# First up phase: four groups on the unnormalised activation, normalised tiles at every second k-tile

## What is computed

```python
def _rmsnorm(x, g):
    y = x32 * lax.rsqrt(jnp.mean(x32 * x32, axis=-1, keepdims=True) + NORM_EPS)
    return (y * g.astype(F32)).astype(x.dtype)

def _conv_ffn(x, w_up, conv_w, conv_b, w_down):
    u = _causal_dwconv(x @ w_up, conv_w, conv_b)      # three taps along the tokens
    gate, up = jnp.split(u, 2, axis=-1)
    return (jax.nn.silu(gate) * up) @ w_down

x = x + mix                                            # attention, ends with @ w_o
x = x + _conv_ffn(_rmsnorm(x, norm_ffn[i]), ffn_w_up[i], ...)
```

## Time and profile before

| what | value |
|---|---|
| median of 3 runs | 819.25 us (818.97 to 820.73) |
| span of the profiled execution | 817.3 us |
| median less span (lead-in and end; the profiled execution has no time of its own beside its span) | 1.95 us |
| TensorE busy | 802.3 us, 98% |
| VectorE busy | 644.4 us, 79% |
| ScalarE busy | 487.0 us, 60% |
| HBM read | 177.27 MB |

### The profile page before, as it was taken

How to read it: one execution, slowest core, us unless ns; L and a number is a source line. 1 busy time by engine, 2 the same in 40 slices (tenths; PEclk the granted TensorE clock), 3 DMA queues, 4 the chain that set the end, 5 groups by cost and what they waited for, 6 DMA issues and landing times.

```text
span 817.3 us, 16917 instructions
## 1 busy us (share of the span) xinstructions
PE 802.3 (98%) x6862; PEld 780.7 (96%) x6862; DVE 644.4 (79%) x1333; ACT 487.0 (60%) x1015; POOL 21.2 (3%) x53
## 2 busy tenths in 40 slices
PE   7999999999999999999999999899999999999998
PEld 7999998999999999999999999889889999999998
DVE  5788887888899887999988786977667896775551
ACT  6754566767767565756554556665655775555440
POOL 1000000000000000000000000700000000000000
PEclk9999999999999999999999999999999999999999
DMA  8777673765565998489998887545334578665540
GB/s 290 260 234 226 200 267 128 235 199 188 189 225 166 324 308 286 144 295 336 361 333 292 288 263 222 167 134 175 120 118 156 156 249 274 207 199 194 194 155 27
DMA packets 150013, 179.44 MB, mean 220 GB/s; under 512 B 5680, under 2 KB 139568, under 8 KB 149936
## 3 DMA queue, kind: packets, MB, share of 16 engines
q1 hardware_dynamic: 147680, 177.22, 65.8%
q10 hardware_dynamic: 1232, 1.11, 0.4%
q0 software_dynamic: 1024, 0.03, 0.1%
HBM read 177.27 MB, written 1.05 MB: 218 GB/s over the span
## 4 chain that ended last, share of the span: by engine, by line
PE 77%; DVE 4%; ACT 2%; issue 1%; DVEq 0%; ACTq 0%
PE bank L1349 24%; PE bank L1352 24%; PE bank L1353 24%; DVE wlo L970 1%; PE bank L1451 1%; PE bank L1439 1%; PE bank L1468 0%; PE bank L1370 0%; PE bank L1402 0%; DVE yb L1010 0%; PE bank L1418 0%; DVE A L1021 0%; ACT B L748 0%; PE bank L1395 0%; ACT sq L768 0%
## 5 line engine op out<-in xcount | busy, mean ns | idle before, releaser
L970 DVE TENSOR_TENSOR wlo<-raw,whi 128x512 fp32r<-128x512 f32 x528 | 342.7, 683 | 69.4 <-ACT whi L727 68.7
L727 ACT ACTIVATE whi<-raw 128x512 fp32r<-128x512 f32 x528 | 307.3, 622 | 97.1 <-PE bank L1353 85.2
L1349 PE MATMUL bank<-A,whi 128*128 128x256 f32 x1264 | 357.3, 283 | 3.4 <-DVE wlo L970 2.6
L1352 PE MATMUL bank<-A,whi 128*128 128x256 f32 x1264 | 350.6, 277 | 0.1
L1353 PE MATMUL bank<-A,wlo 128*128 128x256 f32 x1264 | 350.2, 277 | 0.0
L1349 PEld LDWEIGHTS bank<-A,whi 128*128 128x128 f32 x1264 | 237.7, 188 | 6.5 <-DVE wlo L970 3.5
L1352 PEld LDWEIGHTS bank<-A,whi 128*128 128x128 f32 x1264 | 237.7, 188 | 1.2 <-issue 1.0
L1353 PEld LDWEIGHTS bank<-A,wlo 128*128 128x128 f32 x1264 | 237.8, 188 | 0.0
L1349 PE MATMUL bank<-Hhi,whi 128*128 128x256 f32 x528 | 146.2, 277 | 0.0
L1353 PE MATMUL bank<-Hhi,wlo 128*128 128x256 f32 x528 | 145.9, 276 | 0.0
L1352 PE MATMUL bank<-Hlo,whi 128*128 128x256 f32 x528 | 145.9, 276 | 0.0
(11 more groups left out here) (150 smaller groups left out, 811.0 us busy)
## 6 DMA issues: line engine op xcount, KB each, us to landing
mring<-in_w_mod SPq DMA_DIRECT2D x72, 512.0 KB, 6.4
raw<-in_ffn_w_up SPq DMA_DIRECT2D x22, 1024.0 KB, 5.1
raw<-in_w_gate SPq DMA_DIRECT2D x22, 1024.0 KB, 5.7
raw<-in_w_up SPq DMA_DIRECT2D x22, 1024.0 KB, 6.0
raw<-in_w_down SPq DMA_DIRECT2D x16, 1024.0 KB, 5.4
raw<-in_w_in SPq DMA_DIRECT2D x12, 1024.0 KB, 5.4
raw<-in_moba_w_qkv SPq DMA_DIRECT2D x11, 1024.0 KB, 5.5
raw<-in_ffn_w_down SPq DMA_DIRECT2D x8, 1024.0 KB, 6.2
```

The source lines that it names most:

```text
L727: act.activation(whi[:, i % SPL, k0:k1, 0:width], raw[:, i % RAW, k0:k1, 0:width], ACT.Copy).then_inc(s_whi, 1)
L970: dve.tensor_tensor(lo, raw[:, i % RAW, k0:k1, 0:width], hi.bitcast(F32), ALU.subtract).then_inc(s_wlo, 1)
L1349: pe.matmul(o, hi, xh, start=kg == 0 and not (j and halved(g)), stop=False)
L1352: pe.matmul(o, hi, xl, start=False, stop=False)
```

## The change

Up1 gets the form of the three other phases.

- `RAW_GROUPS` and `RAW_OF` get "up1". The first four groups of up1 (slabs 17 to 20) multiply `B`, 256 columns, filled by "ain" steps behind each residual group of o1.
- The squares of tiles 6 and 7 are one step again, added into `acc` by VectorE; the sum is one step. The second set of fillers is gone.
- The eviction of the first group is deferred to the third k-tile of slab 18, right behind the root's sum. "cg" may now be deferred.
- An unnormalised group is first multiplied by the root, bank to `tmp`, two VectorE instructions. ScalarE's last tap waits for that (`s_scaled`) and all three taps read `tmp`. `s_evicted` is raised where it was, after the taps.
- Normalised tiles: y(0) at k-tile 4 of slab 18, y(1) at k-tile 6, y(2) to y(5) at k-tiles 0, 2, 4, 6 of slab 19, y(6) and y(7) at 0 and 2 of slab 20, each followed by the low part of the tile before. Slab 21 is the first to use them.
- The residuals of down1 also wait for `s_alo` and `s_acc`, since B's low halves and the squares read the same x.

```diff
-RAW_GROUPS = {"up2": 4, "qkv3": 4, "up4": 4}
-RAW_OF = {"up2": 0, "qkv3": 1, "up4": 2}
-LATE_OF = {"up1": 0, "up2": 1, "qkv3": 2, "up4": 3}
+RAW_GROUPS = {"up1": 4, "up2": 4, "qkv3": 4, "up4": 4}
+RAW_OF = {"up1": 0, "up2": 1, "qkv3": 2, "up4": 3}
-WARM = (13, 9)
+WARM = 13
...
-                    if to != "up1":
-                        for n in (c0 // P, c0 // P + 1):
-                            st.put("ain", to, n)
+                    for n in (c0 // P, c0 // P + 1):
+                        st.put("ain", to, n)
                     st.put("sq", to, c0 // C)
...
-                if first and tag not in ("o", "down", "cg"):
+                if first and tag not in ("o", "down"):
                     deferred.append(g)
...
-                if norm == "up1":
-                    st.put("norm", norm)
-                    st.put("warm", 1)
-                    for n in range(KD):
-                        st.put("latey", norm, n)
-                        for m in ([n - 1] if n else []) + ([n] if n == KD - 1 else []):
-                            st.put("latelo", norm, m)
...
+        def up_out(g, i, c0=0, c1=S):
+
+            return tmp[:, (0 if groups[g][1] == "cg" else 2) + i, c0:c1] if g in unnormed else at(g, i, c0, c1)
...
                     if part == 0:
-                        need.wait_ge(s_chunk, chunk_of_group(g))
+                        if g not in unnormed:
+                            need.wait_ge(s_chunk, chunk_of_group(g))
                         need.wait_ge(s_rest, 16)
                         need.wait_ge(s_h1, conv_g[g] // 2)
                         for i in range(2):
                             c = half + 2 * j + i
-                            act.activation(ca[:, sl + i, :], at(g, i), ACT.Identity, bias=cvec[:, 3, c:c + 1],
+                            if g in unnormed:
+                                need.wait_ge(s_scaled, 2 * mul_g[g] - 1 + i)
+                            act.activation(ca[:, sl + i, :], up_out(g, i), ACT.Identity, bias=cvec[:, 3, c:c + 1],
                                            scale=cvec[:, 2, c:c + 1]).then_inc(s_conv0, 1)
...
+                    if part == 0 and g in unnormed:
+                        have_r(ph)
+                        for i in range(2):
+                            dve.tensor_tensor(up_out(g, i), at(g, i), Rr[:, 0, :], ALU.mult).then_inc(s_scaled, 1)
...
                             ins = dve.scalar_tensor_tensor(
-                                out=y[:, part:S], in0=at(g, i, 0, S - part), scalar=cvec[:, 2 - part, c:c + 1],
+                                out=y[:, part:S], in0=up_out(g, i, 0, S - part), scalar=cvec[:, 2 - part, c:c + 1],
...
                 if g in unnormed:
                     need.wait_ge(s_alo, 8 * NORM_OF[ph] + kg + 1)
+                    if ph == "up1":
+                        return Bhi[:, kg, 0:S], Blo[:, kg, 0:S], S
...
-                early = i == plan.first_of["up1"]
-                xh, xl, ncol = here(tag, ph, kg, g, early)
+                xh, xl, ncol = here(tag, ph, kg, g)
```

More of the change, by code:

```diff
@@ L522, in build_program @@
         sq_index = {part: k + 1 for k, part in enumerate(sq_parts)}
-        acc_index = {part: k + 1 for k, part in enumerate(p for p in sq_parts if p[1] > 0 and p != ("up1", 3, 0))}
+        acc_index = {part: k + 1 for k, part in enumerate(p for p in sq_parts if p[1] > 0)}
         conv_g = {g: k for k, g in enumerate(g for g, x in enumerate(groups) if x[1] in ("cg", "cu"))}
@@ L753, in squares @@
                 x_here(ph, 2 * q)
-                if not (ph == "up1" and q == 3):
-                    x_here(ph, 2 * q + 1)
+                x_here(ph, 2 * q + 1)
                 for j in range(2 if ph == "up2" else 1):
@@ L760, in squares @@
                     else:
-                        need.wait_ge(s_acc, acc_index["up1", 2, 0] if ph == "up1" and q == 3 else acc_index[ph, q, j] - 1)
+                        need.wait_ge(s_acc, acc_index[ph, q, j] - 1)
                         o = sq[:, :, :]
[L763 to L767, removed]
+                    if j == 0:
                         act.activation(o, XT[:, 2 * q:2 * q + 2, :], ACT.Square).then_inc(s_sq, 1)
@@ L985, in add_squares @@
             def add_squares(ph, q):
-                if q == 0 or (ph == "up1" and q == 3):
+                if q == 0:
                     return
@@ L997, in late_y @@
                 have_r(ph)
-                k = 8 * LATE_OF[ph] + n
-                if ph == "up1":
-                    emptied(need, res_group("o1", n))
-                    if n >= 4:
-                        need.wait_ge(s_ahi, 8 + n - 3)
-                        need.wait_ge(s_alo, 8 + n - 3)
-                    gain = vec[:, VC["norm_ffn"] + n:VC["norm_ffn"] + n + 1]
-                else:
-                    if n >= 4:
-                        need.wait_ge(s_nhi, 8 * RAW_OF[ph] + n - 3)
-                        need.wait_ge(s_nlo, 8 * RAW_OF[ph] + n - 3)
-                    gain = gcol[:, n:n + 1]
-                dve.scalar_tensor_tensor(out=yb[:, n % 4, :], in0=XT[:, n, :], scalar=gain, in1=Rr[:, 0, :],
+                k = 8 * RAW_OF[ph] + n
+                if n >= 4:
+                    need.wait_ge(s_nhi, 8 * RAW_OF[ph] + n - 3)
+                    need.wait_ge(s_nlo, 8 * RAW_OF[ph] + n - 3)
+                dve.scalar_tensor_tensor(out=yb[:, n % 4, :], in0=XT[:, n, :], scalar=gain_of(ph, n), in1=Rr[:, 0, :],
                                          op0=ALU.mult, op1=ALU.mult).then_inc(s_latey, 1)
@@ L1189, in evict @@
                             need.wait_ge(s_latey, n + 1)
+                            need.wait_ge(s_alo, 8 + n + 1)
+                            need.wait_ge(s_acc, acc_index["up1", 3, 0])
                         elif ph == "down2":
@@ L1303, in _, with here @@
             need = Once(pe)
-            def here(tag, ph, kg, g, high=False):
-                if high:
-                    need.wait_ge(s_ahi, 8 * NORM_OF[ph] + kg + 1)
-                    return Ahi[:, kg, :], Alo[:, kg, :], S
+            def here(tag, ph, kg, g):
                 if tag in ("o", "ot"):
@@ L1349, in multiply @@
                     pe.matmul(o, hi, xh, start=kg == 0 and not (j and halved(g)), stop=False)
-                    if early:
-                        here(tag, ph, kg, g)
                     pe.matmul(o, hi, xl, start=False, stop=False)
@@ L1355, in multiply, with warm @@
                     ins.then_inc(s_chunk, 1)
-            def warm(k):
+            def warm():
                 need.wait_ge(s_const, 3)
-                for _ in range(WARM[k]):
+                for _ in range(WARM):
                     pe.matmul(banks[T_BANK][:, 0:P], meanf[:, :], meanf[:, :], start=True, stop=True)
@@ L1365, in norm @@
                 need.wait_ge(s_const, n_const)
-                late = ph == "up1"
                 for j in range(2 if ph == "up2" else 1):
-                    need.wait_ge(s_acc, acc_index[ph, 2 if late else 3, j])
+                    need.wait_ge(s_acc, acc_index[ph, 3, j])
                     for t in range(2):
-                        ins = pe.matmul(b[:, j * S:(j + 1) * S], meanf[:, :], acc[:, j, t, :], start=t == 0, stop=t == 1 and not late)
-                if late:
-                    need.wait_ge(s_sq, sq_index[ph, 3, 0])
-                    for t in range(2):
-                        ins = pe.matmul(b[:, 0:S], meanf[:, :], sq[:, t, :], start=False, stop=t == 1)
+                        ins = pe.matmul(b[:, j * S:(j + 1) * S], meanf[:, :], acc[:, j, t, :], start=t == 0, stop=t == 1)
                 ins.then_inc(s_sums, 1)
```

27 lines of the change are left out of this document (14 added, 13 removed).

## The result

The changed kernel takes 826.94 us (median of 5 runs, 826.70 to 827.84) where the kernel before took 820.32 beside it (818.97 to 820.73): ratio 1.0087, 95% interval 1.0071 to 1.0102. It is slower by some 7 us, outside the range given.

The account below looks back on a forecast made before the run. TensorE, 98% busy, bounds the kernel, but VectorE's list in up1 sets the end: the seam's 5.8 us come back in the fifth slab, so 819.25 + 0.2 = 819.5 us, range 815.8 to 822.2.

Parts of the forecast that it names:

- The seam: From o1 to up1, B products follow O without a gap, at 127.27, removing 5.82 us without product work.
- rival D: At the tile 5 stall the clock grant falls to 1.2 GHz: +3 us, 822.5; chance 0.08.
- the stall at tile 5: In up1's fifth slab TensorE waits 3.3 us for normalised tile 5, ready at 158.5.
- VectorE's list: VectorE's uninterrupted work in up1 from the root to normalised tile 5: 21.7 us, setting the end.
- The root: Sum matmul in up1's second slab at 134.7; VectorE starts scaling at 136.8.
- Rival B: VectorE passes up1's fifth slab without being late; the seam's 3.4 to 3.8 us stay: 815.7; chance 0.14.
- B slabs: Each of up1's first four slabs, multiplied from B, takes 5.75 us, between ends 5.44 and 5.8.
- rival C: ScalarE's round trips lengthen VectorE's list in up1; with 2.0 us more, 821.5; chance 0.16.
- The waits inside the list: VectorE waits in up1: 1.0 us behind the silu table load, 0.4 for ScalarE's copy in the third group.
- A: VectorE gives back the whole seam gain in up1's fifth slab: 819.5, range 818.2 to 820.9; chance 0.62.
- Banks of the fourth group, weights: After up1's fifth slab: bank emptied about 165.0, wanted 167; seventh-slab weights 3 us early, later loads' lateness hidden.
- The sum: Sixth up1 slab starts at 161.3 to 161.5 against 161.20: change +0.2 us, total 819.5.

Follow-up runs that it names:

- experiment 1: Changed kernel with the bank turn begun at 0 instead of 2, so up1 starts on banks 0 and 1: 823.0 us, ratio 1.0043.
- experiment 2: Changed kernel with the bank turn begun at 1 instead of 2, so up1 starts on banks 2 and 3: 821.87 us, ratio 1.0030.
- experiment 3: Changed kernel, banks as they are, plus 13 filler matmuls ahead of up1's first product: 824.84 us, ratio 1.0069.
- experiment 6: Kernel of experiment 2 without VectorE's convolution taps for the four unnormalised groups (output not the reference's): 819.92 us, ratio 1.0002.
- the table variant: Kernel of experiment 1 with ScalarE's silu table loaded right behind the root, ahead of the first copy: 822.83 us, ratio 1.0045.
- experiment 8: Kernel before without its nine filler matmuls at the o1 to up1 seam: 821.79 us, ratio 1.0026.
- experiment 4: Kernel of experiment 1 with six unnormalised groups in up1 instead of four: 824.19 us, ratio 1.0057.
- experiment 5: Kernel of experiment 2 with up1's normalised tiles made at every k-tile instead of every second: 821.66 us, ratio 1.0031.
- experiment 7: Kernel of experiment 5 with the low half of up1's hidden tiles computed on GpSimd instead of VectorE: 822.70 us, ratio 1.0041.
- the shifted B: Kernel of experiment 5 with the rows of B 272 columns apart instead of 258: 822.35 us, ratio 1.0034.

## Why the prediction failed, point by point

**The seam (the step that failed first).** "The stream could go on at 127.27" took the o3 to up4 seam as price list. Up4 begins with the first pair of banks, which o3's last group does not hold; up1 begins with the pair that o1's last group holds. I did not look up who owned the bank. Experiments 1 and 2 change nothing else and the wait is gone. It costs 3.3 us (130.59 where 127.27 was forecast), and the first fall of the clock came with it.

**The clock (the second).** The forecast took no fall, and gave rival D a chance of 0.08 although it named the place, the stall at tile 5. That fall came in the profiles of the change and of every kernel here whose stall at tile 5 stayed (experiments 1, 2, 3, 6 and the table variant); in experiment 6 a wait of 2.32 us was enough. Its price was overstated: matmuls start 0.21 us apart instead of 0.12 over 3.41 us, so some 1.4 us of work are lost and not 3; experiment 3 gives 1.3. The Trainium skill (TensorE: Matmul & The Clock Gate, Part 1), which the prediction weighed at D, says that an idle array drops to half rate, and the traces agree: 0.50 in or behind waits of 3.17, 3.07 and 3.06 us., on which I leaned, show a wait of 1.93 us only, and experiment 8 shows a fall within waits of 1.19 and 2.03. "The granted clock is 1.00 throughout" was also read too far: the first 4.70 us have no record.

**VectorE's list (right).** 21.7 us were forecast and 22.3 measured, 22.3 again in experiment 2 (136.68 to 158.98). The root came when it was to come, once the bank was put right: 136.68 in experiment 2, 136.8 forecast. The stall at tile 5 was to be 3.3 and was 3.07 and 3.06. The 0.6 us too little lies in the taps: four from `tmp` take 1.76, where 1.64 was taken from the earlier trace rows, and two with a split between them 0.87 each, so that twelve come to 5.2 rather than 4.7. Rival B, that the list is not late, is thereby out. The Trainium skill (VectorE: DVE Perf Modes, The TRN2 errata), by which a source in SBUF should make the taps cheaper, is not borne out: 0.44 each from `tmp` against 0.41 from a bank.

**B slabs (right).** 5.75 us forecast, 5.71 measured for a slab at full clock, between the ends 5.44 and 5.8.

**The round trips (rival C, half right).** The waits inside the list came to 1.0 (weights at 147.64) and 0.34 (the third group's copy), as forecast. But experiment 6 shows that they stand just beneath the list: C was no addition to A here, but is what most of A turns into when VectorE is relieved (2.7 of 4.7 us).

**Banks of the fourth group, weights (right).** No wait for banks or weights follows in up1, and the sixth slab's lag is down1's lag.

**The sum.** The forecast's own sum has one small slip: it took 161.20 for the start of the sixth slab before, from 5.44 us a slab, where the trace has 161.29, because the slab behind a reset takes 5.53; the +0.2 should have been +0.1. The rest is followed along VectorE, whose list sets the end: it starts at 141.40 instead of 136.8, 4.6 late, which is 3.3 for the bank (130.59 less 127.27) and 1.3 for the first fall. The list is 0.6 longer. From tile 5 to the sixth slab TensorE takes 4.0 us (163.76 to 167.77) where 2.9 was forecast (158.5 to 161.4): 1.1 for the second fall. With the 0.2 of the forecast that makes 6.5, against 6.48 measured. With the bank put right (experiment 2) the list starts on time, at 136.68, and down1 1.92 us late: 0.2 forecast, 0.6 for the list, 1.1 for the fall.

The third fall, in qkv3 at 532.85, is in a stretch with the same instructions as before. It is in the profile (mean clock 0.994) but, by the mean clock of 0.996, not in the median run of the change. The kernel before has such runs too: with a mean clock of 0.998 it takes 820.7 to 822.05 where it takes 819.2 at 1.000, and about one run in five is at 0.998 or less. What decides over it was not found. In experiment 2's profile there is such a fall at 528.43; of that kernel's 2.6 us over the kernel before, 1.9 are there at down1. Its two runs with a mean clock of 0.997 and 0.998 took 821.14 and 821.40, about that much over, and the four with 0.996 took 821.76 to 823.40, so the rest fits a second fall, though only one of these runs has a trace that shows it.

**Why nothing was gained.** The change wins 5.8 us of TensorE's time at the seam and asks VectorE for scaling, taps and tiles, one behind the other, in a stage where it works 9.91 of 11.00 us. Experiments 4, 5 and 6 move the deadline, the order and the amount: in the median only the last is clearly below experiment 2, and only by 1.95 us for 4.7 us of work. That nothing can be had here is not shown, though. Experiment 7 reaches the sixth slab 0.8 us ahead of the kernel before and loses it where matmuls start 117.8 ns apart; without knowing why they do, that stays open.

## What to carry to other kernels

If another seam serves as a price list, compare not only its instructions but the buffers at both sides: which bank the last group holds and which the first one takes. A stall may only be moved into a stage whose second engine has room; where it was 90% busy here, the stall came back, as a wait for whatever stood last in its list. And look at what fillers do before they are removed together with the wait that they fill: a stall of 2 to 3 us brought a further 1.1 to 1.3 us through the clock. And before profiles of two variants are compared, look how far each profiled run lies from its own median.

## What the runs showed of the hardware that was not expected

- A fall of the granted clock lasted 3.41 us (the change) or 6.83 (experiments 1 and 8 and the table variant). It did not come with waits of 1.39, 1.26 and 0.97 us that lie 7 us apart (experiment 4). It came behind a wait of 2.32 us (experiment 6); with the same wait for a bank it came in one profile (2.41 us, experiment 5) and not in two others (2.42 us, experiment 7 and the shifted B).
- Two GpSimd subtractions of 128x256 (1.67 to 2.15 us) slow VectorE's subtractions beside them: a split of 683 ns takes up to 1231 ns, and the mean over the whole stretch goes from 684 to 749.
- The same fp32 matmul on 256 columns mostly costs 113.3 ns from A and 119 from B in up1 (117.8 with the rows of B 272 columns long). But the price from A is not fixed: in stretches of 4 us (o1 of the kernel before) to over 60 us (down1 in experiment 7) it is 117.8 at a granted clock of 1.00 and without waits.
- A lag of VectorE can outlive a whole phase: that of experiment 4 passed through down1 without a wait of TensorE over 0.1 us and surfaced at 321.76, 149 us after the last wait of up1.
